# Rows to and from eight experts by one-hot products on the chip, in place of tables in DRAM, with experts ordered by load

## The reference, cut to what matters

```python
def moe_swiglu(x, w_router, w_gu, w_down):
    ...
    logits = (xt @ w_router).astype(jnp.float32)
    top_v, top_i = lax.top_k(logits, TOP_K)          # TOP_K = 2
    top_w = jax.nn.softmax(top_v, axis=-1)
    gates = jnp.sum(jax.nn.one_hot(top_i, N_EXPERTS, dtype=jnp.float32) * top_w[..., None], axis=1)
    for e in range(N_EXPERTS):                       # 8
        h = xt @ w_gu[e]                             # 1024 x 5632
        y = (jax.nn.silu(h[:, :D_EXPERT]) * h[:, D_EXPERT:]) @ w_down[e]   # 2816 x 1024
        out = out + gates[:, e:e + 1].astype(xt.dtype) * y
...
        x = layer_norm(DEEP_ALPHA * x + h, ln_g[layer, 1], ln_b[layer, 1])
```

## Time and profile before

| | |
|---|---|
| median of three runs | 1212.91 us |
| lowest, highest | 1212.02, 1213.2 us |
| profiled execution, its own time | 1211.24 us |
| its span, first to last instruction | 1209.5 us |
| mean granted TensorE clock | 0.997 |
| PE, PEld, DVE, ACT, POOL busy, share of the span | 98, 79, 34, 24, 8% |
| read from HBM, written to it | 353.21, 15.34 MB |
| chain that ended last: PE's products at L1543 | 91% |

### The profile page before, as it was taken

One profiled execution on the slowest core, in us unless ns is written; L12 is line 12 of the kernel. 1 busy time (PEld: TensorE's weight loads), 2 busy tenths in 40 slices (PEclk: granted clock), 3 DMA queues, 4 the chain that ended last, 5 costly groups with the idle time before them and its releaser, 6 DMA issues.

```text
span 1209.5 us, 35715 instructions
## 1 busy us (share of the span) xinstructions
PE 1184.1 (98%) x16815; PEld 955.9 (79%) x16815; DVE 416.7 (34%) x537; ACT 295.4 (24%) x482; POOL 100.0 (8%) x141
## 2 busy tenths in 40 slices
PE   9999999999999999999999999999999999999996
PEld 8998998888888897766887787986676587786585
DVE  5876855666654685403011011011011030030032
ACT  5885444555543465200000000000000000000001
POOL 4024300300000200200000000000000000000100
PEclk9999999999999999999999999999999999999998
DMA  9835012679655543899999999999999999999992
GB/s 311 287 118 196 2 36 70 199 289 382 210 189 194 175 140 118 328 397 399 418 409 398 418 406 397 417 402 394 411 407 392 402 411 394 391 413 418 409 411 108
DMA packets 110841, 370.94 MB, mean 307 GB/s; under 512 B 10064, under 2 KB 53824, under 8 KB 83040
## 3 DMA queue, kind: packets, MB, share of 16 engines
q1 hardware_dynamic: 100144, 345.01, 74.0%
q0 software_dynamic: 6256, 20.71, 4.7%
q10 hardware_dynamic: 4288, 2.87, 0.7%
HBM read 353.21 MB, written 15.34 MB: 305 GB/s over the span
## 4 chain that ended last, share of the span: by engine, by line
PE 93%; DVE 2%; DMA 2%; POOL 1%; ACT 1%; issue 1%; DVEq 0%; SPq 0%; POOLq 0%; ACTq 0%
PE ps L1543 91%; DMA over<-in_moe_w_down 1%; ACT ps L654 1%; PE ps L1901 0%; DMA x<-in_x 0%; PE ps L1674 0%; PE ps L1554 0%; POOL lnrs L486 0%; DVE x L1035 0%; POOL DT L512 0%; DVE x L1045 0%; DVE x L1515 0%; POOL dist L446 0%; DVE xT_both L991 0%; DVE x L1005 0%
## 5 line engine op out<-in xcount | busy, mean ns | idle before, releaser
L1481 DVE TENSOR_TENSOR actE<-sgE,ps 128x1536 f32<-128x1536 f32 (+1 forms) x16 | 32.9, 2057 | 589.2 <-PE ps L1543 492.3
L1543 PE MATMUL ps<-xT_both,hi 128*128 128x256 f32 (+1 forms) x896 | 221.3, 327 | 2.5 <-DVE xT_both L991 2.5
L1543 PE MATMUL ps<-raw,xgT 128*32 128x256 f32 (+1 forms) x4272 | 219.3, 361 | 2.1 <-issue 0.8
L1543 PE MATMUL ps<-over,xgT 128*32 128x256 f32 (+1 forms) x4272 | 220.0, 361 | 0.8 <-issue 0.8
L1543 PEld LDWEIGHTS ps<-raw,xgT 128*32 128x32 f32 x4272 | 162.0, 110 | 54.6 <-issue 2.0
L1543 PEld LDWEIGHTS ps<-over,xgT 128*32 128x32 f32 x4272 | 161.2, 110 | 54.0 <-issue 2.1
L983 DVE TENSOR_TENSOR lo<-raw,hi 128x2048 fp32r<-128x2048 f32 x62 | 144.3, 2330 | 96.4 <-ACT hi L635 96.4
L1543 PE MATMUL ps<-xT_both,lo 128*128 128x256 f32 x624 | 174.4, 280 | 0.0
L1543 PEld LDWEIGHTS ps<-xT_both,hi 128*128 128x128 f32 x896 | 150.7, 190 | 18.1 <-issue 2.9
L635 ACT ACTIVATE hi<-raw 128x2048 fp32r<-128x2048 f32 x62 | 118.8, 1917 | 112.9 <-PE ps L1543 109.3
L917 ACT ACTIVATE sgE<-ps 128x1536 f32<-128x1536 f32 (+1 forms) x16 | 16.8, 1051 | 437.7 <-PE ps L1543 437.7
(11 more groups left out here) (317 smaller groups left out, 1130.6 us busy)
## 6 DMA issues: line engine op xcount, KB each, us to landing
raw<-in_moe_w_gu SPq DMA_DIRECT2D x59, 1024.0 KB, 19.6
over<-in_moe_w_gu SPq DMA_DIRECT2D x59, 1024.0 KB, 21.2
raw<-in_moe_w_down SPq DMA_DIRECT2D x43, 1024.0 KB, 15.0
over<-in_moe_w_down SPq DMA_DIRECT2D x38, 1024.0 KB, 16.3
raw<-in_moe_w_gu SPq DMA_DIRECT2D x60, 384.0 KB, 11.4
over<-in_moe_w_gu SPq DMA_DIRECT2D x60, 384.0 KB, 10.8
raw<-in_ffn_w_gu SPq DMA_DIRECT2D x44, 512.0 KB, 4.6
raw<-in_dn_w_in SPq DMA_DIRECT2D x32, 512.0 KB, 8.8
```

What stands on the lines that cost most here:

```text
L1481: dve.tensor_tensor(actE[:, 0:g_ * n_].rearrange("p (g t b) -> p g b t", g=g_, b=32), sgE[:, 0:g_ * n_].rearrange("p (g b t) -> p g b t", ...
L1543: return pe.matmul(dst, lhsT, rhs, start=start, stop=stop)
```

## The change

- **Order.** PE's counts of tokens per expert are copied (`loads`), DVE ranks the experts by load (`route_order`) and writes the order as integers. Expert 0 stays first, and the experts behind it come by falling load; SyncE reads each one's number into a register and addresses the weights with it. FULL = 8, so `groups(s)` is 3 for each of the eight: every expert is computed with 96 rows.
- **Rows in.** For each next expert DVE makes the one-hot of slots (`mark_slots`), PE multiplies it with x (`dispatch`) after the expert's 11th unit, and ACT and DVE copy half of the result each into one of two `xgT` buffers.
- **Rows out.** DVE makes the one-hot of lanes with the gates in it (`mark_lanes`), PE transposes it before the 7th unit (`turn_places`), ACT copies it. The result of expert s - 1 is multiplied with it inside expert s, one block of tokens before down unit 5, one before down unit 8 (`give_back`), and DVE adds it to `acc` (`add_spread`).
- **Gone.** The tables `xe`, `ys` and `ys_late`, their clearing, the indirect DMAs, the gathers and stores, `turn_xg` and `add_picked`, and the row arithmetic.
- **Ring.** 16 slots. Units 0 to 3 go to `raw` slots, units 4 to 7 to four new ones that lie in buffers which attention has done with (`more` over xT_both, `over_q` over qT, `over_k` over kT2), then the two other `raw` ones and the six of `over`.
- **Weights' layout.** All experts take gate/up rows as (k p).
- The late part is rewritten in the same manner; it isn't entered with these inputs.

The diff, cut to its core:

```diff
+    FULL = 8
...
-    RING = RAW + 2 * CUT + 1
+    RING = RAW + 2 * CUT + 4
...
+            more = sb("more", [P, 2, UNIT], where=a)
...
-        mgu_v = moe_gu[0].rearrange("e (p k) n -> e p k n", k=KD)
-        mgu_first = moe_gu[0][0].rearrange("(k p) n -> p k n", p=P)
+        mgu_v = moe_gu[0].rearrange("e (k p) n -> e p k n", p=P)
...
+        FREED = 4
+        EXTRA = 4
+        LEFT = RAW - FREED
+
+        def raw_place(i):
+            return i if i < FREED else i - EXTRA
+
+        def is_raw(i):
+            return i < FREED or FREED + EXTRA <= i < RAW + EXTRA
...
+            return (more[:, 0, :], more[:, 1, :], over_q[:, :], over_k[:, :])[i - FREED]
...
+                elif n >= RING:
+                    sp_.wait_ge(unit_used, done(n - RING))
+                elif is_raw(i):
+                    sp_.wait_ge(lo_ready, U_MOE - RAW + raw_place(i) + 1)
+                elif i < FREED + 2:
+                    sp_.wait_ge(unit_used, U_Q + 4)
+                elif i < FREED + EXTRA:
+                    sp_.wait_ge(sc_mm, 4)
                 else:
-                    sp_.wait_ge(unit_used, done(n - RING))
+                    sp_.wait_ge(unit_used, U_O + 1 + min((i - RAW - EXTRA) // 2, CUT - 1) + 1)
...
+            for l in range(PER_E):
+                expert_unit(l, 0)
+            sp_.wait_ge(order_here, 1)
+            for s in range(1, E):
+                e = sp_.value_load(order[0:1, s:s + 1], min_val=0, max_val=E - 1)
+                for l in range(PER_E):
+                    expert_unit(PER_E * s + l, e)
...
-            pool.dma_start(xe.rearrange("(k r) d -> r k d", r=P), zeros.unsqueeze(1).to_broadcast([P, rows, D])).then_inc(xe_clear, 16)
...
-                    pool.indirect_dma_start(xe, bass.IndirectOffsetOnAxis(ap=row[:, i, b, :], axis=0), x[:, b, :], None
-                                            ).then_inc(dispatched, 16)
-            pool.wait_ge(dispatched, 32 * NB)
-
...
-                    pool.dma_start(xg[32 * a:32 * a + 32, :, :], rows[a]).then_inc(gathered, 16)
-
...
-                    for k in range(2):
-                        pool.indirect_dma_start(picked[:, b, k, :], None, source,
-                                                bass.IndirectOffsetOnAxis(ap=row[:, 2 + 2 * i + k, b, :], axis=0)
-                                                ).then_inc(picked_here[b], 16)
...
+            def take_rows(s, g_):
+                act.wait_ge(xg_turned, 2 * s + 1)
+                copy(*rows_of(s, 0, 32 * g_)).then_inc(xg_here, 1)
+
+            def take_places(s, g_):
+                act.wait_ge(onehT_mm, s + 1)
+                copy(onehT[:, s % 2, 0:NB * g_ * P], ps[:, 6:8, :].rearrange("p b n -> p (b n)")[:, 0:NB * g_ * P]).then_inc(onehT_here, 1)
+
...
-                act.wait_ge(y_there, free)
-                copy(ysb[:, :, :], ps[:, 6:8, :].rearrange("p b n -> p (b n)")[:, 0:GROUPS * 256].rearrange("p (g n) -> p g n", g=GROUPS)
-                     ).then_inc(y_out, 1)
...
+                if s:
+                    act.wait_ge(spread, 2 * s)
...
+                copy(ysb[:, 0:g_, :], src).then_inc(y_out, 1)
...
             for s in range(E):
-                if s == 1:
-                    act.wait_ge(dispatched, 32 * NB)
-                    copy(x[:, :, :], x[:, :, :], scale=ALPHA).then_inc(x_scaled, 1)
-                taken(s, False, PER_E * s + 2 * KD - 2)
-                if s == 0:
-                    act.wait_ge(onehT_mm, 1)
-                    copy(onehT[:, :, :, :].rearrange("p b g t -> p (b g t)"),
-                         ps[:, 6:8, :].rearrange("p b n -> p (b n)")[:, 0:NB * GROUPS * P]).then_inc(y_out, 1)
-                taken(s, True, PER_E * s + GU_E - 1)
+                take_places(s, groups(s))
                 if s < E - 1:
-                    returned(PER_E * s + PER_E - 1, 64 * s, s + 2, ys_v[s])
...
+            def mark_slots(cap, column):
+                for b in range(NB):
+                    last = dve.tensor_scalar(oneh[:, b, 0:cap], iota[:, 0:cap], column[:, b, :], None, ALU.is_equal)
+                last.then_inc(oneh_here, 1)
+
+            def mark_lanes(s, g_, places, weights):
+                if s:
+                    dve.wait_ge(onehT_mm, s)
+                for b in range(NB):
+                    last = dve.tensor_scalar(ohl[:, b, 0:g_, :], lane[:, 0:g_, :, :].rearrange("p g a r -> p g (a r)"),
+                                             places[:, b, :], weights[:, b, :], ALU.is_equal, ALU.mult)
+                last.then_inc(ohl_here, 1)
+
+            def take_rows(s, g_):
+                dve.wait_ge(xg_turned, 2 * s + 2)
+                dve.tensor_copy(*rows_of(s, 1, 32 * g_)).then_inc(xg_here, 1)
+
+            mark_slots(CAP, place[:, :, 0:1])
+            dve.wait_ge(pos_mm, 2)
+            dve.tensor_copy(loads[:, :], ps[:, 4, 2 * E:3 * E]).then_inc(load_here, 1)
+            take_rows(0, groups(0))
...
+            def route_order():
+                dve.wait_ge(load_here, 1)
+                step(dve.scalar_tensor_tensor(out=key[:, :], in0=loads[:, :], scalar=16.0, in1=ebias[:, :], op0=ALU.mult, op1=ALU.add))
+                step(dve.tensor_tensor(bigger[:, :, :], key[:, :].unsqueeze(1).to_broadcast([P, E, E]),
+                                       key[:, :].unsqueeze(2).to_broadcast([P, E, E]), ALU.is_gt))
+                step(dve.tensor_reduce(turn_of[:, :], bigger[:, :, :], AX.X, ALU.add))
+                link(dve.tensor_scalar(roomE[:, :], turn_of[:, :], FULL - 0.5, 32.0, ALU.is_lt, ALU.mult))
+                step(dve.tensor_tensor(mine[:, :, :], turn_of[:, :].unsqueeze(1).to_broadcast([P, E, E]),
+                                       eidx[:, :].unsqueeze(2).to_broadcast([P, E, E]), ALU.is_equal))
+                link(dve.scalar_tensor_tensor(out=excess[:, :], in0=loads[:, :], scalar=32.0 - CAP, in1=roomE[:, :],
+                                              op0=ALU.add, op1=ALU.subtract))
+                step(dve.tensor_tensor(bigger[:, :, :], mine[:, :, :], eidx[:, :].unsqueeze(1).to_broadcast([P, E, E]), ALU.mult))
+                link(dve.tensor_reduce(cmax[:, :], excess[:, :], AX.X, ALU.max))
+                step(dve.tensor_reduce(orderf[:, :], bigger[:, :, :], AX.X, ALU.add))
+                dve.tensor_copy(order[:, :], orderf[:, :]).then_inc(order_here, 1)
...
                 dve.tensor_copy(cint[:, :], cmax[:, :]).then_inc(route_here, 1)
...
+                for i in range(2):
+                    link(dve.tensor_tensor(top[:, i, :, :], pick[:, i, :, :], gw[:, :, 2 + i:3 + i].to_broadcast(each), ALU.mult))
+                settle()
+                step(dve.tensor_tensor(gates, top[:, 0, :, :], top[:, 1, :, :], ALU.add))
+                step(dve.tensor_tensor(each_mine[:, :, :, :], mine[:, :, :].unsqueeze(1).to_broadcast([P, 2 * NB, E, E]),
+                                       by_expert[:, :, :].unsqueeze(2).to_broadcast([P, 2 * NB, E, E]), ALU.mult))
+                step(dve.tensor_reduce(by_turn[:, :, :], each_mine[:, :, :, :], AX.X, ALU.add))
...
+            def add_spread(s, b, last=False):
+                dve.wait_ge(spread, 2 * s + b + 1)
+                got = ps[:, 4 * b:4 * b + 4, 0:256] if last else ps[:, 0:4, 256 * b:256 * b + 256]
+                sum_ = acc[:, b, :].rearrange("p (a n) -> p a n", a=4)
+                if s == 0:
+                    dve.scalar_tensor_tensor(out=sum_, in0=x[:, b, :].rearrange("p (a n) -> p a n", a=4), scalar=ALPHA, in1=got,
+                                             op0=ALU.mult, op1=ALU.add).then_inc(spread_added, 1)
+                    return
+                dve.wait_ge(spread_added, 2 * s + b - 1)
+                if last:
+                    dve.scalar_tensor_tensor(out=sum_, in0=got, scalar=1.0, in1=sum_, op0=ALU.mult, op1=ALU.add,
+                                             accum_out=lnsum[:, b:b + 1]).then_inc(spread_added, 1)
+                    dve.wait_ge(spread_added, 2 * s + b + 1)
...
-                                              in1=x[:, b, :], op0=ALU.mult, op1=ALU.add))
+                    dve.tensor_tensor(sum_, got, sum_, ALU.add).then_inc(spread_added, 1)
...
+            route_order()
             route_gates()
             for s in range(E):
+                mark_lanes(s, groups(s), by_turn[:, 0:NB, s:s + 1], by_turn[:, NB:2 * NB, s:s + 1])
+                if s < E - 1:
+                    mark_slots(32 * groups(s + 1), by_turn[:, 0:NB, s + 1:s + 2])
+                    take_rows(s + 1, groups(s + 1))
+                hidden(s, False, groups(s), PER_E * s + 2 * KD - 1)
+                hidden(s, True, groups(s), PER_E * s + GU_E - 1)
                 if s:
...
-                    add_picked(b, i)
+                    for b in range(NB):
...
+            def dispatch(s, g_):
+                cap = 32 * g_
+                pe.wait_ge(oneh_here, s + 1)
+                for i in range(2):
+                    for q in range(4):
+                        for b in range(NB):
```

(96 more changed lines are left out.)

392 lines of the change are left out of this document (140 added, 252 removed).

## The result

The changed kernel takes 1268.85 us (median of four runs, 1267.48 to 1270.02), the kernel before 1213.06 us beside it: 55.8 us more, a ratio of 1.0461 (95% interval 1.0443 to 1.0479). Its profiled execution took 1270.02 us, span 1268.2.

A forecast was written before the change was run, and what follows sets the result against it. PE was taken as the bound: 1211.24 us profiled, plus 52.0 for seven experts' added blocks at 7.43 each, minus 0.7 of weight waits, plus 1.67 to the runs' median, gives 1264.2 us, range 1254 to 1283.

The forecast's parts named there:

- less than 1% behind: Expert stage: PE is the bound, with DMA keeping up barely, less than 1% behind it.
- rival A: Expert stage's weight ring: weights set the pace, so less transfer makes the kernel faster, 1181 us; 3 in 100.
- Parts 1 and 2: PE, inside experts: dispatch adds 3.65 us of weight loads without fringes, the one-hot's transposes 0.80 us, seven times each.
- Parts 3 and 4: PE, inside experts: give_back in two halves adds 2.5 us, array shape changes 0.12 us for each of four blocks.
- Parts 5 to 9: Removed transfers give -0.7 us; early slots, SP's wait for the order, DVE and ACT work, and the tail give 0.
- within some 5 us: Sign in the changed profile: a gate/up unit lands within some 5 us of its issue, against 24.5 us before.
- B: PE in the expert stage: added products fit into gaps, so no change; needs 52 us of slack; 1 in 100.
- C: PE in each expert: five new waits on ACT and DVE, 1.3 us each, make 45 us more, 1309; 5 in 100.
- D: SP's weight DMAs: register addresses make issues slow, at 2.5 us each 7 x 13 more, 1355; 3 in 100.
- my high bound: PE's inserted blocks: the array runs empty at every shape change, 8 x 0.38 = 3.0 us per expert, giving 1283.

The follow-up runs named there:

- e1: Changed kernel with the 16 products that pick the rows of experts 1 to 7 issued twice in a row; 1291.23 us, one run.
- e2: Kernel before with 16 useless dispatch-sized products on PE before the first down unit of experts 0 to 6; 1238.18 us against 1213.41.
- e7: Kernel before without the products of every expert's third group of 32 rows, all weights and tables still moving; 1205.33 us against 1217.68.
- e3: Changed kernel with both halves of give_back issued as one block before down unit 5; 1264.89 us, ratio 1.0422.
- e11: Changed kernel as it is, run again on a third chip; 1266.26 us, ratio 1.0397 to the kernel before at 1218.24 us.
- e12: Changed kernel with a ring of 13 slots in place of 16, on one chip with the unaltered changed kernel; 1269.16 us, ratio 1.0417.
- e4: Changed kernel with FULL = 2, so the six experts with the smallest loads use 64 rows, not 96; 1181.68 us, ratio 0.9737 to the kernel before.

## Why the prediction was right

- **What bounds.** PE's pace, right in both kernels (e1, e2). My reading that the weights were "less than 1% behind" was wrong in its sense: they were 1.7% slower (e7), and the ring's head start hid it until the last expert. That PE set the time to the end is in part luck of the count: with more experts, or less in the ring, rival A would have come in, by this account (no run tries it). The pace of units told who sets the time now; it doesn't tell how long that can last. The landing times by stretch (e7) would have told it before any run.
- **Parts 1 and 2.** Dispatch was taken at 3.77 us with its fringes and measured at 3.85; the transposes at 0.92 and measured at 0.92.
- **Parts 3 and 4, the one mis-sized term.** Two halves of give_back were 2.74 us in the sum and are 3.24. The 0.11 us of the transposes was reckoned over their own pace of 0.80 us, while dispatch and give_back stand in the sum with their weight loads alone. Over its weight loads a transpose block costs 0.28 us, and a half of give_back, a block of another shape, 0.44 us over 1.18. e3 takes out one leaving and coming back and gains 0.32 us. Seven times 0.5 us is 3.5 of the 4.6 us by which the median passed my 1264.2; e11, the same kernel on another chip, passed it by 2.1.
- **The total of the stage.** 52.0 us were expected of PE's blocks, 56.1 measured; the waits for weights went, as forecast, while the gaps of "issue" on PE stand at 4.2 us from 520 to 1253, in e11 at 1.8, and in the kernel before at 2.4 from 520 to 1200.
- **Parts 5 to 9.** Nothing of the removed transfers came back as time beyond the 0.7 us of waits, the early slots gave nothing (e12), the order's wait on SP and the register addresses cost nothing that PE saw, DVE and ACT stayed off the path. Wrong was the landing time, "within some 5 us": it is 10.1; why a unit takes that long with slack in the transfers was not tried.
- **The rivals.** A, B, C and D didn't come. What A looks like stands in e7 and e4, and the changed kernel has nothing of it.
- **The Trainium skill's two rules.** The rule that a change of tiling mode drains the engine (TensorEngine Tiling (Array Packing), Key Properties) agrees with the traces in kind: PEld is idle ahead of every such block; whether the array itself runs empty they don't show. The price for a pair of changes, over the block's weight loads, is 0.20 to 0.44 us, not the full 0.76 us (two products of 0.38) of my high bound. The rule that weight-load busy time, beside the share of peak arithmetic, is the better measure (the Trainium skill, Perfetto Trace Analysis, Identifying the Most-Contended Engine) would have misled if taken by the weight loads alone: PEld was busy 65% of an expert that had no time to give.

The whole effect of the change as it stands is that it moves work from transfers, which PE hid, to PE. Its gain comes only when FULL is lowered: sorting lets six experts use 64 rows, which takes a third off PE's products there and leaves the weights as the bound.

## What to carry to other kernels

When two resources both look full, compare the spacing of equal pieces of work in stretches where one of the two is known to be slack; then put a known amount of useless work on the suspected one, and take a third off it. The three together say who sets the pace and by how much the other is behind. A deep ring that starts full can hide a slower stream for the whole run, so read its landing times stretch by stretch, as a reserve that is being used up, and cost every block between streams of another tile shape with its own idle edges.

## What the runs showed of the hardware

The 944 products of the dense SwiGLU, which no kernel here changes, take either 176.7 or 179.1 us, at a granted clock of 1.00 both times. The chain of waits of the changed kernel's first profile and of the same kernel in e11 has both:

```profile
215.83 179.09 PE ps L1525 x944
```

```profile
215.85 176.72 PE ps L1525 x944
```

Nine profiles show the shorter and five the longer; it goes by the execution, not by the kernel, and its cause was not tried. It is 2.4 us, as much as a single comparison here can tell.

The kernel before took 1213.1 to 1213.4 us in two of the measurements and 1217.7 and 1218.2 us in two others, on other chips, while the changed one stayed at 1266.3 to 1268.9. Its weights run so close to PE that a slower stream would show there first; against that, the 84.2 us of a weight-bound expert without tables were the same on three chips. No profile of the slower executions was taken, so that stays open.
